# The sample stage of a hybrid decoder step: rows of both branches on 128 partitions, in four column groups

## The reference, cut to what matters

```python
def _sample_mix(q_a, k_a, v_a, q_b, k_b, v_b, logf, pool_a_k, ..., page_table, slopes, lam):
    ka = concat([gather_pages(pool_a_k, page_table), k_a], axis=1)      # 512 past + 4 new keys
    ...                                                                 # va, kb, vb alike
    F_past = cumsum(gather_pages(pool_b_logf, page_table), axis=1)
    F_new = F_past[:, -1:, :] + cumsum(logf, axis=1)
    o_a = _diff_attn(q_a, ka, va, q_pos, k_pos, slopes, lam)            # softmax map 0 - lam * softmax map 1
    o_b = _forgetting_attn(q_b, kb, vb, F_new, F_k, q_pos, k_pos)       # scores + F_q - F_k
```

## Time and profile before

| | |
|---|---|
| median of 3 runs | 3007.55 us (3004.43 to 3007.67) |
| profiled execution | 3005.72 us, its span 3004.1 us |
| mean granted TensorE clock | 0.956 |
| busy over the span | PE 92%, DVE 52%, ACT 32%, POOL 7% |
| sample stage | from 2290.8 to 2554.7 us |

### The profile page before, as it was taken

How to read it: one execution, slowest core, us unless ns; L and a number is a source line. 1 busy time by engine, 2 the same in 40 slices (tenths; PEclk the granted TensorE clock), 3 DMA queues, 4 the chain that set the end, 5 groups by cost and what they waited for, 6 DMA issues and landing times. The chain is left out here.

```text
span 3004.1 us, 34561 instructions
## 1 busy us (share of the span) xinstructions
PE 2761.6 (92%) x12679; PEld 2030.6 (68%) x12679; DVE 1576.6 (52%) x2448; ACT 974.9 (32%) x1570; POOL 196.0 (7%) x176
## 2 busy tenths in 40 slices
PE   6699999994999989999997999899997888699999
PEld 1488888872777767777775777677774332588886
DVE  2421224654345546667772777677775332555553
ACT  0411112224222247771001777644442221322221
POOL 1000001220012200000000100000001000001000
PEclk9799999995999999999998999999998998799999
DMA  5545545533554365654436666335634541444431
GB/s 200 190 160 186 217 153 170 149 90 125 167 154 142 105 188 130 152 140 119 123 104 159 133 145 148 72 78 116 121 73 141 175 144 52 171 130 135 136 119 58
DMA packets 284848, 410.90 MB, mean 137 GB/s; under 512 B 78379, under 2 KB 169643, under 8 KB 275469
## 3 DMA queue, kind: packets, MB, share of 16 engines
q1 hardware_dynamic: 281314, 383.23, 45.1%
q10 hardware_dynamic: 2338, 25.71, 2.2%
q0 software_dynamic: 1056, 0.13, 0.1%
HBM read 272.75 MB, written 136.24 MB: 136 GB/s over the span
## 5 line engine op out<-in xcount | busy, mean ns | idle before, releaser
L1252 DVE TENSOR_REDUCE max_neg_top<-max_s_ps 128x1 f32<-128x1024 f32 (+7 forms) x384 | 349.0, 913 | 170.2 <-PE max_s_ps L1310 115.0
L459 PE MATMUL proj_z<-proj_w_hi,h_hi 128*128 128x512 f32 x768 | 302.0, 393 | 0.0
L459 PE MATMUL proj_z<-proj_w_hi,h_lo 128*128 128x512 f32 x768 | 299.3, 390 | 0.0
L459 PE MATMUL proj_z<-proj_w_lo,h_hi 128*128 128x512 f32 x768 | 298.9, 389 | 0.0
L1626 ACT ACTIVATE att_b_pf<-att_b_s_ps 128x1024 f32<-128x1024 f32 (+2 forms) x160 | 141.0, 899 | 144.6 <-PE att_b_s_ps L1680 77.3
L1219 ACT ACTIVATE max_s_ps<-max_s_ps,max_neg_top 128x128 f32<-128x128 f32 (+2 forms) x192 | 161.0, 839 | 72.0 <-DVE max_neg_top L1252 71.5
L1334 PE MATMUL max_z<-gate_w_hi,h_hi 128*128 128x512 f32 (+1 forms) x432 | 178.3, 413 | 3.2 <-PEq L662 3.2
L1334 PE MATMUL max_z<-gate_w_lo,h_hi 128*128 128x512 f32 (+1 forms) x432 | 177.7, 411 | 0.0
L1443 ACT ACTIVATE att_a_pf<-att_a_s_ps,head_bias 128x1024 f32<-128x1024 f32 (+3 forms) x160 | 158.3, 989 | 58.7 <-PE att_a_s_ps L1520 32.3
L1334 PE MATMUL max_z<-gate_w_hi,h_lo 128*128 128x512 f32 (+1 forms) x432 | 176.7, 409 | 0.0
L459 PE MATMUL proj_z<-gate_w_hi,h_hi 128*128 128x512 f32 (+1 forms) x432 | 173.5, 402 | 0.0
(11 more groups left out here) (331 smaller groups left out, 5834.6 us busy)
## 6 DMA issues: line engine op xcount, KB each, us to landing
proj_w_raw<-in_w_in SPq DMA_DIRECT2D x144, 256.0 KB, 4.2
mrg_mix<-scratch_mixes SPq DMA_DIRECT2D x16, 1024.0 KB, 4.8
ada_w<-in_w_ada SPq DMA_DIRECT2D x8, 1536.0 KB, 9.7
scratch_w_split<-proj_w_hi ACTq DMA_DIRECT2D x6, 2048.0 KB, 6.7
scratch_w_split<-proj_w_lo ACTq DMA_DIRECT2D x6, 2048.0 KB, 13.0
gate_w_hi<-scratch_w_split SPq DMA_DIRECT2D x48, 256.0 KB
gate_w_lo<-scratch_w_split SPq DMA_DIRECT2D x48, 256.0 KB
map_qm<-scratch_q_hi SPq DMA_DIRECT2D x48, 256.0 KB
```

The lines of the kernel that those rows point to most:

```text
L459: ins = nc.tensor.matmul(out, left(*lt), right(*rt), start=first and n == 0, stop=last and n == len(terms) - 1)
L1252: nc.vector.tensor_reduce(neg_top[:, kh, u, qt:qt + 1], s_ps[:, x % SLOTS, 0:width[x]], AX.X, ALU.max, negate=True).then_inc(max_done, 1)
```

## The change

Rows of both branches now share 128 partitions. Partition 32 * (2e + c) and up hold group (e, c): branch c (0 is A, 1 is B) and the head half e. Each group contracts only the two chunks of keys that its heads need, and writes its own 32 partitions of one bank. For the values, group (e, c) contracts the key pages 2q + e, and the halves are added by the pick. The probabilities are turned by products with `turn`, a selection matrix scaled by the reciprocal sums, so that rows of both halves come out in one order. `pick` accumulates over all sequences in `ps_x` and is copied once at the end. `q_blk` is made by multiplying the queries with a mask. Keys are turned into four banks. The order of VectorE's turn changes. The constants are built in the modulation stage, stored to a DRAM tensor `smp_const` (128 x 2496 float32), and loaded with one DMA on ScalarE's queue at the start of the sample stage. `v_s` has 128 partitions with zeros. The small products with the new keys change as the large ones of the scores do, and `choose` is the copy of the selection that `prepare` held before. The core of the diff:

```diff
 (constants)      nc.gpsimd.memset(k.logf[:], 0.0)
+                nc.gpsimd.memset(k.v_s[:], 0.0)
 (modulation)
+                sample_constants_made(k, const, pool)       # 7 iotas, 13 affine_selects with waits, fills
+                sample_constants_ended(k, const, pool)      # 3 affine_selects, behind VectorE's part
...
-                act.wait_ge(rows_stored, 64)
+                act.wait_ge(const.done, 3)
+                act.dma_start(k.smp_const, const.tile[:]).then_inc(rows_stored, 16)
+                act.wait_ge(rows_stored, 80)
...
                 last.then_inc(pos_done, 1)
+                sample_constants_spread(k, const, dve)      # some 40 VectorE instructions, widest 128 x 512
                 dve.wait_ge(b_loaded, 16)
 (sample, VectorE)
+                def prepare(b, s):
+                    for c in range(2):
+                        v.tensor_tensor(q_blk[s][:, c, :, :].rearrange("p a (x t) -> p a x t", t=NT),
+                                        k.qT_s[:, c, :, ds(b * NT, NT)].unsqueeze(2).to_broadcast([P, 4, 8, NT]),
+                                        at.unit.unsqueeze(3).to_broadcast([P, 4, 8, NT]), ALU.mult)
+                    v.tensor_copy(pick_b[s][:].unsqueeze(1), at.pick_f[:, ds(b, 1), :, :]).then_inc(S["prepared"], 1)
+                def biased(b):
+                    dve.wait_ge(S["s_done"], b + 1)
+                    v.tensor_tensor(sc[:, 0:PAST], ps_s[:], at.past, ALU.add)
+                    v.tensor_tensor(sc[:, PAST:KEYS].unsqueeze(1), ps_n.unsqueeze(1), at.new[:, ds(b, 1), :], ALU.add)...
+                    v.tensor_reduce(neg_max[:], sc[:], AX.X, ALU.max, negate=True).then_inc(S["max_done"], 1)
...
                 def body(i, s, first, last):
                     b = i * 2 + s
-                    if not first:
-                        own_columns(b - 1)
-                    if not last:
-                        k_turned(b + 1)
-                    if not first:
-                        add(b - 1)
-                        if not last:
-                            prepare(b + 1, 1 - s)
...
-                    if not last:
-                        biased(b + 1)
+                    if not first:
+                        if not last:
+                            dve.wait_ge(S["s_done"], b)
+                            prepare(b + 1, 1 - s)
...
+                        choose(b, s)
+                    turning(b, s, first)                      # reciprocal, turn = order * recip
+                    if not first:
+                        own_columns(b - 1, ...)
+                    if not last:
+                        k_turned(b + 1, (0, 2))
+                    turned(b, first)                          # pT, pT_new copies
+                    if not last:
+                        k_turned(b + 1, (4, 6))
+                        biased(b + 1)
                     out_w_low(k, dve, i, s)
 (sample, ScalarE)
-                    act.wait_ge(S["s_done"], b + 1)
-                    a.activation(sc[:, 1, 0:PAST], ps_s[:, 1, :], ACT.Copy).then_inc(S["past_b"], 1)
...
-                    for c in range(2):
-                        a.activation(pr[:, c, :], sc[:, c, :], ACT.Exp, bias=neg_max[:, c:c + 1],
-                                     accum_out=sums[:, c:c + 1]).then_inc(S["p_done"], 1)
+                    a.activation(pr[:], sc[:], ACT.Exp, bias=neg_max[:], accum_out=sums[:]).then_inc(S["p_done"], 1)
+                act.dma_start(const[:], k.smp_const).then_inc(S["const_in"], 16)
 (sample, TensorE; GROUPS are the four (e, c, rows 32 * (2e + c) and up))
-                    for c in range(2):
-                        for p in range(4):
-                            mm(ps_s[:, c, :], q_blk[s][:, c, p, :], kT[:, c, p, :], start=p == 0, stop=p == 3 and c == 0)
-                    mm(ps_s[:, 1, :], pick_b[s][:], f_rel[:], start=False, stop=True)
+                    for q in range(2):
+                        for e, c, r in GROUPS:
+                            mm(ps_s[r, :], q_blk[s][:, c, 2 * e + q, :], kT[:, c, 2 * e + q, :], start=q == 0, stop=q == 1 and c == 0)
+                    for e, c, r in GROUPS[1::2]:
+                        mm(ps_s[r, :], pick_b[s][:, e, :], f_rel[:], start=False, stop=True)
...
+                def turn_p(b):
+                    pe.wait_ge(S["turn_done"], b * 2 + 2)
+                    for g in range(NPG):
+                        mm(ps_p[:, g * 2 * SR:(g + 1) * 2 * SR], pr[:, g * PG:(g + 1) * PG], turn[:], start=True, stop=True)
+                    mm(ps_p[0:SR, NPG * 2 * SR:], pr[:, PAST:KEYS], turn[:], start=True, stop=True).then_inc(S["pt_ready"], 1)
 (turn: turn_k 0 to 4, turn_p, turn_k 4 to 8, pick, scores, values)
-                        for g in range(NPG):
-                            mm(ps_o[:, c, :], pT[:, c, g, :], kv[s][2 + c][:, g, :], start=g == 0, stop=False)
-                        done = mm(ps_o[:, c, :], pT_new[:, c, :], k.v_s[:, c, :], start=False, stop=True)
+                    for q in range(2):
+                        for e, c, r in GROUPS:
+                            mm(ps_o[r, :], pT[:, 2 * q + e, c, :], kv[s][2 + c][:, 2 * q + e, :], start=q == 0, stop=q == 1 and e == 1)
+                    for e, c, r in GROUPS[0:2]:
+                        done = mm(ps_o[r, :], pT_new[:, c, :], k.v_s[:, c, :], start=False, stop=True)
```

More of the change, by code:

```diff
@@ L1719, in _, with sample_views @@
                 turn(N - 1)
+SMP = {}
+for _name, _cols in (("own", W), ("past", PAST), ("new", NB * SR), ("sel", 2 * NB * SR), ("pick_f", NB * 2 * SR), ("pick_h", 2 * SR),
+                     ("order", 2 * SR), ("unit", 4 * 8), ("tri", SR)):
+    SMP[_name] = (sum(b - a for a, b in SMP.values()), sum(b - a for a, b in SMP.values()) + _cols)
+NSMP = max(b for _, b in SMP.values())
+def sample_views(tile):
+    at = {n: tile[:, a:b] for n, (a, b) in SMP.items()}
+    m = Store()
+    m.own, m.past, m.order, m.tri = at["own"], at["past"], at["order"], at["tri"][0:SR, :]
+    m.new = at["new"].rearrange("p (b k) -> p b k", b=NB)
+    m.sel = at["sel"].rearrange("p (c b k) -> p c b k", c=2, b=NB)
+    m.pick_f = at["pick_f"].rearrange("p (b e r) -> p b e r", b=NB, e=2)
+    m.pick_h = at["pick_h"].rearrange("p (e r) -> p e r", e=2)
+    m.unit = at["unit"].rearrange("p (a x) -> p a x", a=4)
+    return m
@@ new lines, in sample_constant_buffers @@
+def sample_constant_buffers(k, ctx):
+    sb, _, sem = tools(k, ctx, "smpc")
+    m = Store()
+    m.tile = sb("tile", [P, NSMP])
+    m.at = sample_views(m.tile)
+    m.row = sb("row", [P, 4], I32)
+    m.col, m.head_a, m.head_b = sb("col", [P, PAST], I32), sb("head_a", [P, W], I32), sb("head_b", [P, W], I32)
+    m.tok, m.place, m.x = sb("tok", [P, SR], I32), sb("place", [P, 2 * SR], I32), sb("x", [P, 4 * 8], I32)
+    m.bits, m.part = sb("bits", [P, 8], I32), sb("part", [P, 12])
+    m.slope, m.key, m.match = sb("slope", [P, 1]), sb("key", [P, SR]), sb("match", [P, 3, SR])
+    m.pool_step, m.dve_step, m.made, m.spread, m.done, m.filled = (
+        sem(n) for n in ("pool_step", "dve_step", "made", "spread", "done", "filled"))
+    return m
@@ L1722, in out_weights, with sample_constants_ended @@
+def sample_constants_ended(k, m, pool):
+    g, at, step = k.nc.gpsimd, m.at, Tally(m.done)
+    pool.wait_ge(m.spread, 1)
+    pattern = [[-1, NB], [1, NB], [0, NT]]
+    for ap, fill in ((at.new, NEG), (at.sel[:, 0, :, :], 0.0), (at.sel[:, 1, :, :], 0.0)):
+        ap = ap.rearrange("p b k -> p (b k)")
+        step.inc(g.affine_select(out=ap, in_=ap, compare_op=ALU.is_equal, fill=fill, base=0, pattern=pattern, channel_multiplier=0))
 def out_weights(k, ctx):
@@ L1763, in sample @@
     TURNS = NB // 2
+    GROUPS = [(e, c, slice(SR * (2 * e + c), SR * (2 * e + c) + SR)) for e in range(2) for c in range(2)]
     with ExitStack() as ctx:
@@ L1794, in sample @@
[L1794 to L1803 removed]
+        f_rel, f_new = sb("f_rel", [P, PAST]), sb("f_new", [P, SR])
+        q_blk = [sb(f"q_blk{s}", [P, 2, 4, SR]) for s in range(2)]
@@ L1833, in next_v @@
                     load_out_w(k, sp, i, s)
-                for what in range(2):
-                    load(0, 0, what)
-                    load(1, 1, what)
+                load(0, 0, 0)
+                load(1, 1, 0)
+                load(0, 0, 1)
+                load(1, 1, 1)
                 for s in range(2):
@@ L1973, in own_columns @@
[L1973 to L1984 removed]
+                v.tensor_copy(f_new[0:HB, :], ps_n[0:HB, :]).then_inc(S["fn_copied"], 1)
```

331 lines of the change are left out of this document (161 added, 170 removed).

## The result

The changed kernel takes 2876.72 us (median of 4 runs, 2875.75 to 2879.42) against 3007.61 us of the kernel before (4 runs, 3004.43 to 3009.11): a ratio of 0.9565, 95% interval 0.9554 to 0.9577, 131 us less. I had predicted 2912 us in a range of 2880 to 2980.

A forecast was written before the change was run, and what follows sets the result against it. TensorE was taken to pace the sample stage. Stage 236.6 to 148 us, 6.6 us earlier start and 1 us store cost gave 94 us less: 3005.7 − 94 = 2912 us, range 2880 to 2980 (8 in 10).

The forecast's parts named there:

- TensorE, part by part: Sample-stage turn on TensorE: two instructions overlap; scores 5.8, values 4.8, picks 1.3, probabilities 1.1, key transposes 3.8, sum 16.8 us.
- The sum: Sample stage: first scores 7.8, first turn 12.5, six turns 109.2, last part 18.5, together 148 us against 236.6.
- The chain through VectorE: VectorE and ScalarE from one turn's scores to `turn`: 6.2 us, hidden because TensorE arrives last at 6.7 us.
- My own case: Sample-stage products overlap two instructions at a time: 18.2 us a turn with the clock, 2912 us; chance 50%.
- The clock: Sample-stage turns: lower granted clock adds 1.4 us a turn, half of the 2.8 that the slow turn cost.
- rival 2: Sample-stage products overlap four at a time: turn of 15 us, stage 122 us, 120 us less, 2886 us; chance 18%.
- rival 3: Granted clock stays at 1.2 GHz through the sample stage: 33.6 us a turn, 3038 us; chance 5%.
- The loads: SP's queue in a sample-stage turn: 13.1 us of SP work, 12.9 us of transfers; a floor, not a new limit.
- No overlap (rival 1): Sample-stage products run one after another wherever they write: 26.2 us a turn, 2976 us; chance 24%.
- Start and modulation: Scores start at 2311.5 us, 6.6 us sooner; modulation-stage constant building hidden, its store costing 1 us.
- The two extra banks: Key transposes in the sample stage: take the wait on kT copies out of the first half; transposes 3.8 us.

The follow-up runs named there:

- experiment 1: Changed kernel with the large score and value products issued column group by column group instead of alternating between groups; 2874.01 us, ratio 0.9553.
- Experiment 4: Changed kernel with VectorE's `out_w_low` of the turn before placed ahead of `biased`, where VectorE waits for scores; 2869.16 us, ratio 0.9538.
- experiment 9: The version with three edits, but SP reads no page numbers and sequence b takes pages 4b to 4b + 3; 2853.33 us, ratio 0.9485.
- the version with three edits: Changed kernel with `out_w_low` moved ahead of `biased`, sequence 2's keys loaded before sequence 1's values, and five loads reusing page numbers; 2860.85 us, ratio 0.9504.
- Experiment 5: Changed kernel with the third sequence's keys and the first output weights loaded ahead of the second sequence's values; 2870.12 us, ratio 0.9544.
- x_one_so: Changed kernel with all large score and value products written to partitions 0 to 31, one column group; 2945.97 us, ratio 0.9793.
- experiment 3: Changed kernel with two PSUM banks for the turned keys instead of four; 2907.21 us, ratio 0.9669.
- x_k2_early: Changed kernel with the keys of sequence 2 loaded ahead of the values of sequence 1; 2870.12 us, ratio 0.9544.

## Why the prediction was wrong, point by point

**The step that failed** is in "TensorE, part by part": "If instructions start in program order, the second half of a product has to wait for the first, and what can run beside it is only the first half of the next product: two instructions at a time". The rows of the changed kernel show four at a time for scores and values, and experiment 1 shows why: the column groups do not share one order. Everything that hung on it was too dear: scores 5.8 against 2.7 us (2354.47 to 2357.15), values 4.8 against 2.8, picks 1.3 against 0.9, together 11.9 of my 16.8 us where 6.4 were measured.

The page TensorE: Matmul & The Clock Gate of the Trainium skill, Part 3, says that matmuls are strictly first in, first out, in start and end. The trace disagrees between column groups: a small product starts at 2356.21, the second instruction of a forget product ahead of it in the program at 2356.64. The Trainium skill's page TensorEngine Tiling (Array Packing), Overview, promises up to 4×; the trace agrees with 7.03 / 1.91 = 3.7. I had weighed the two pages and leant on the one that resembled my own argument.

**The sum.** By its terms, forecast and measured (cut where each group of scores ends, to some 0.1 us): first scores 7.8 and 2.9 us; first turn 12.5 and 9.9; six turns 109.2 and 89.7; the last part 18.5 and 12.8. The differences, 4.9, 2.6, 19.5 and 5.7, are the 32.7 us between 148 and 115.3. With the bound of four at a time I had 5.5 + 10.5 + 90 + 16 = 122, so that rival was 7 us too dear, in the first scores and in the last part. That its 90 us for the six turns meet the 89.7 measured is luck: its full-clock turn was 1.1 us too long (13.9 against 12.81), and the wait of 6.62 us for keys was not in it. Two slips of addition change nothing: the parts of the first turn sum to 12.3, not 12.5, and 2912 with 20 us each way is 2892 to 2932, not 2895 to 2935.

**The chain through VectorE: right, and with four at a time decisive.** I wrote that TensorE "would be there at 4.6 and wait for VectorE", 6.2 us after the scores. The wait in the trace is 1.36 us (6.2 − 4.6 = 1.6 by those numbers). Experiment 4 confirms the cause, `out_w_low`. My own case called the chain hidden, which was true only of the wrong mode.

**The clock.** I added 1.4 us a turn to mine and 1.1 to rival 2. The six turns take 89.7 us, of which 6.6 are the wait for keys: 83.1. At full clock five of them would take 12.81 and the one without a wait for `turn` 11.45: 75.5. So the lower clock cost 7.6 us, 1.3 a turn. More than half of it, 4.2 us, lies in the turn behind the wait for keys (15.65 us from 2331.52 to 2347.17, granted clock 0.69), so the size came out near for a reason I did not have. The lower clock throughout (rival 3) did not come; over 2350 to 2420 us the granted clock is 0.95.

**The loads: the floor was right, the early order was missed.** SP's 13.1 us a turn "nearly touch 13.9"; experiment 9 shows that this is what holds the version with three edits. What I did not see is the order at the start: SP issues the keys of the third sequence behind the values of two sequences and the weights, and a faster TensorE turns that into a wait of 6.62 us with the lower clock behind it. The trace of the kernel before shows the same order and nearly the same time, further down SP's queue than the earlier trace rows:

```profile
2324.11 1.92 SPq L1821 DMA_DIRECT2D smp_k_a<-in_cache_a_k  x4
```

I had reckoned the queue as a rate and never held this row against the time at which TensorE would ask. With two products at a time it would have asked at some 2311.5 + 7.8 + 12.5 + 4.8 = 2336.6 us by my terms, behind the 2331.5 at which the keys are there; with four at a time it asks at 2324.9. So this wait, too, follows from the step that failed. Experiment 5 gets 6.6 us back.

**No overlap (rival 1)** was mis-sized: 2976 us forecast, 2946 in x_one_so. Of the 30 us, 6 × (26.2 − 23.1) = 19 lie in the middle turns: no loss of clock (1.2 us), small products inside the scores (8.7 us instead of 9.6), and picks that x_one_so left in four groups (0.9). The other 11 us I have not split.

**Start and modulation: right.** Scores start 2.1 us sooner than the 2311.5 forecast, 1.5 of it upstream. The addition in the modulation stage moved by 0.04 us, where I had allowed 1. The two extra banks, which I costed only as "takes the wait on kT copies out of the first half", are worth 30 us (experiment 3); I had given them no size.

**The range.** It reached rival 2 at 2886 with 6 us beyond it, and rival 2 itself was 9 us too high. A range that ends close to a rival's centre leaves half of that rival outside.

## What to carry to other kernels

If products have few output columns, write consecutive ones to different column groups: float32 products in four groups took 3.7 times less than in one, and with equal counts in all groups the order did not matter here. When the bound engine becomes twice as fast, redo the sum for all that was hidden behind it: here it uncovered in turn a VectorE step that nobody was waiting for, the order of the first loads, and the queue's time for reading page numbers, and each of the first two cost 7 us, the third 10. A DMA share near 1 does not prove that transfers are the limit; take the issuing away and see.

## What was not expected of the hardware

- Matmul instructions of different column groups overtake each other (2356.21 against 2356.64 us in the changed kernel, and all of experiment 1), but not without limit: with the values group by group, fourteen instructions ahead of it, the fourth group started 0.90 us late.
- Loads to 64 partitions instead of 128 moved 254 GB/s at a DMA share of 0.95; full ones 355 to 389.
- The granted clock of the changed kernel alternates between turns (1.00 and 0.88 by turns of 12.81 and 14.43 us), with a wait of 1.3 to 1.5 us in each. In x_k2_early, waits of 1.3 and 1.4 us went with turns at 1.00 throughout, and so did turns without a wait in experiments 4 and 9. What decides between the two levels in a turn with such a wait stays open.
